# A mixture-of-experts stage: every other weight block issued from ScalarE's queue

## The reference

```python
D_EXPERT = 7 * D_MODEL // 2

def swiglu(t, w_gate, w_up, w_down):
    return (jax.nn.silu(t @ w_gate) * (t @ w_up)) @ w_down

def moe_swiglu(t, router, w_gate, w_up, w_down):
    logits = (t @ router).astype(jnp.float32)
    top_logits, top_idx = lax.top_k(logits, TOP_K)
    gates = jax.nn.softmax(top_logits, axis=-1)
    combine = jnp.sum(jax.nn.one_hot(top_idx, N_EXPERTS, dtype=jnp.float32) * gates[..., None], axis=1)
    out = jnp.zeros_like(t)
    for e in range(N_EXPERTS):
        out = out + combine[:, e:e + 1].astype(t.dtype) * swiglu(t, w_gate[e], w_up[e], w_down[e])
    return out
```

## Time and profile before

| | us |
|---|---|
| median of three executions | 3119.86 (3119.49 to 3123.53) |
| the profiled execution | 3112.41 |
| its span | 3110.6 |
| the first expert begins (TensorE's first unit) | 2019.2 |
| TensorE busy in the span | 2810.8 (90%) |
| DVE, ScalarE busy in the span | 1739.6, 1419.2 |
| DMA engines' share on SP's queue, whole span | 49.9% |

### The profile page before, as it was taken

How to read it: one execution, slowest core, us unless ns; L and a number is a source line. 1 busy time by engine, 2 the same in 40 slices (tenths; PEclk the granted TensorE clock), 3 DMA queues, 4 the chain that set the end, 5 groups by cost and what they waited for, 6 DMA issues and landing times.

```text
span 3110.6 us, 38240 instructions
## 1 busy us (share of the span) xinstructions
PE 2810.8 (90%) x15246; PEld 2269.4 (73%) x15246; DVE 1739.6 (56%) x1787; ACT 1419.2 (46%) x1567; POOL 29.7 (1%) x40
## 2 busy tenths in 40 slices
PE   6989889999887998767679998799999999999997
PEld 4865378854776998667469996687778777777786
DVE  3234265510444775432345445387878878788786
ACT  3234143300343554311134444376766767676675
POOL 0000000000010000000000000000000000000000
PEclk9999999999999999877689999899999999999998
DMA  7447122211332444300015441298989989898895
GB/s 310 183 183 271 54 83 107 90 66 71 112 122 75 150 158 154 112 1 1 16 66 189 159 181 56 95 353 298 351 322 330 343 304 358 302 345 328 324 348 214
DMA packets 84932, 589.78 MB, mean 190 GB/s; under 512 B 9936, under 2 KB 10064, under 8 KB 21328
## 3 DMA queue, kind: packets, MB, share of 16 engines
q1 hardware_dynamic: 83376, 576.16, 49.9%
q10 hardware_dynamic: 1440, 11.93, 1.0%
HBM read 587.01 MB, written 1.05 MB: 189 GB/s over the span
## 4 chain that ended last, share of the span: by engine, by line
PE 82%; DVE 9%; ACT 4%; issue 2%; DMA 2%; ACTq 0%; DVEq 0%; POOL 0%; SPq 0%; POOLq 0%
PE banks L449 24%; PE banks L443 19%; PE banks L444 19%; PE banks L445 19%; DMA ring<-in_stream 2%; DVE ring_rounded L505 1%; ACT ring_rounded L495 1%; DVE ring_rounded L2611 1%; PE banks L2449 1%; DVE rstd L696 1%; DVE activations L1256 0%; PE banks L772 0%; ACT scratch L836 0%; DVE nmax L808 0%; DVE aT L709 0%
## 5 line engine op out<-in xcount | busy, mean ns | idle before, releaser
L444 PE MATMUL banks<-ring_rounded,activations_rounded 128*128 128x512 f32 x1344 | 530.7, 395 | 0.0
L505 DVE TENSOR_TENSOR ring_rounded<-ring,ring_rounded 128x2048 fp32r<-128x2048 f32 (+3 forms) x150 | 302.7, 2022 | 394.3 <-ACT ring_rounded L495 393.4
L444 PE MATMUL banks<-aT_rounded,ring_rounded 128*128 128x256 f32 (+1 forms) x1552 | 500.8, 323 | 0.0
L495 ACT ACTIVATE ring_rounded<-ring 128x2048 fp32r<-128x2048 f32 (+3 forms) x150 | 253.7, 1695 | 324.1 <-PE banks L445 309.3
L444 PEld LDWEIGHTS banks<-aT_rounded,ring_rounded 128*128 128x128 f32 x1552 | 301.3, 194 | 20.8
L443 PE MATMUL banks<-aT_rounded,ring_rounded 128*128 128x256 f32 x960 | 276.5, 288 | 20.9 <-DVE aT_rounded L718 11.6
L444 PEld LDWEIGHTS banks<-ring_rounded,activations_rounded 128*128 128x128 f32 x1344 | 254.7, 190 | 53.6
L445 PE MATMUL banks<-aT_rounded,ring_rounded 128*128 128x256 f32 x960 | 274.8, 286 | 0.0
L2611 DVE TENSOR_TENSOR ring_rounded<-ring,tables_rounded 128x2048 fp32r<-128x2048 f32 x112 | 253.6, 2287 | 27.8 <-ACT tables_rounded L2534 27.5
L2611 DVE TENSOR_TENSOR ring_rounded<-ring,aT_rounded 128x2048 fp32r<-128x2048 f32 x112 | 254.2, 2288 | 19.1 <-ACT aT_rounded L2534 18.9
L2534 ACT ACTIVATE tables_rounded<-ring 128x2048 fp32r<-128x2048 f32 x112 | 215.1, 1921 | 107.5 <-DMA ring<-in_stream 96.7
(11 more groups left out here) (290 smaller groups left out, 5075.3 us busy)
## 6 DMA issues: line engine op xcount, KB each, us to landing
ring<-in_stream SPq DMA_DIRECT2D x491, 1024.0 KB, 5.3
ring<-in_stream SPq DMA_DIRECT2D x48, 704.0 KB, 5.5
ring<-in_stream SPq DMA_DIRECT2D x28, 768.0 KB, 6.4
activations<-in_rpb ACTq DMA_DIRECT2D x2, 1536.0 KB, 6.3
tables<-in_tab_b ACTq DMA_DIRECT2D x1, 2436.0 KB, 8.6
tables<-in_tab_a ACTq DMA_DIRECT2D x1, 2304.0 KB, 8.4
hT<-in_h ACTq DMA_DIRECT2D x1, 2048.0 KB, 15.5
ring<-in_stream SPq DMA_DIRECT2D x4, 512.0 KB, 6.2
```

Source lines behind the costliest of these rows:

```text
L444: pe.matmul(out, exact(upper), exact(w_lower), start=False, stop=False)
L495: act.activation(exact(upper), w, ACT.Copy).then_inc(g.s["act_pieces"], 1)
L505: dve.tensor_tensor(exact(w), w, rounded(upper), ALU.subtract).then_inc(g.s["dve_pieces"], 1)
```

## The change

ScalarE's `split(u)` for even u now issues the DMA of unit n = u + 1, once TensorE has finished unit u - 6, which is unit n - 7. The two waits of `split` have changed places: first TensorE's, then the issue, then the landing of unit u. SyncE issues one unit more ahead of the loop (unit 5), and in the loop only the even units, 6 to 46. The line numbers of `experts_act` behind the new lines move by five.

```diff
         def split(u):
 
-            act.wait_ge(g.expert_in[u % EXPERT_RING], 16 * (u // EXPERT_RING + 1) + it * (16 * UNITS // EXPERT_RING))
             if u >= UPPERS:
                 act.wait_ge(s["pe_experts"], g.at("unit", u - UPPERS) + it * Q)
             else:
                 act.wait_ge(s["pe_experts"], g.at("unit", UNITS + u - UPPERS) - Q + it * Q)
+            if u % 2 == 0:
+
+                n = u + 1
+                src = g.io["stream"][bass.ds(e * ES + (g.expert_base + n // 2), 1), :, UNIT:2 * UNIT]
+                act.dma_start(g.units[n % EXPERT_RING], src.rearrange("a p n -> p (a n)")).then_inc(g.expert_in[n % EXPERT_RING], 16)
+            act.wait_ge(g.expert_in[u % EXPERT_RING], 16 * (u // EXPERT_RING + 1) + it * (16 * UNITS // EXPERT_RING))
             act.activation(exact(g.upper[u % UPPERS]), g.units[u % EXPERT_RING], ACT.Copy).then_inc(s["act_split"], 1)
@@ experts_sp
-    for u in range(AHEAD):
+    for u in range(AHEAD + 1):
 
         sp.wait_ge(*g.moment(("used", base - 1 - (base - 1 - u // 2) % RING)))
         sp.dma_start(g.units[u], g.io["stream"][base + u // 2, :, UNIT * (u % 2):UNIT * (u % 2) + UNIT]).then_inc(g.expert_in[u], 16)
@@
         it = r * NE + e
-        for u in range(AHEAD, UNITS + AHEAD):
+        for u in range(AHEAD + 1, UNITS + AHEAD, 2):
             if u < EXPERT_RING:
```

## The result

| | before | after |
|---|---|---|
| median | 3121.38 us (four executions, 3119.49 to 3123.53) | 3174.12 us (four, 3157.82 to 3175.79) |
| ratio | | 1.0157, 95% interval 1.0123 to 1.0192 |
| the profiled execution, its span | 3112.41, 3110.6 us | 3175.79, 3174.0 us |

By the ratio the changed kernel is slower by 49 us (38 to 60 us); the two medians lie 53 us apart. The direction was forecast, the size was not: 3285 us with a range from 3180 us was too high.

What follows compares the result with a forecast made beforehand. TensorE was taken to set the pace, with ScalarE right behind the transfers. Chained odd transfers cost 23.2 us an expert, times eight 185.6, less 6.6 reserve: 179 us, giving 3285 us (range 3180 to 3370).

Steps and rivals of the forecast that it cites:

- The mechanism: In ScalarE's list, each odd unit's issue waits for the previous odd unit's landing, forming a chain of 7.58 us steps.
- h: On ScalarE, hold from an odd unit's landing to the next odd issue: 0.10 plus some 0.20 us, 0.3 us a step.
- Rival A: Odd and even transfers keep alternating in the expert stage, so not slower: 3120 us within 5 us; chance 0.09.
- Rival B: ScalarE's issues wait for the running ACTIVATE's end: steps of 7.5 us, landings near 5.3 us, 3318 us; chance 0.08.
- 21 steps x 7.58: One expert's odd transfers, all chained and nearly coinciding with even ones: 159.2 us before corrections.
- about two steps run alone: In TensorE's 11.5 us of pauses an expert, two steps are 2.0 us cheaper each: -4.1 us.
- that is where they settle: Odd and even transfers on the two queues stay nearly coincident, odd 0.5 us behind even, at steps of 7.58 us.
- rival C: The chain slips only in part of each expert, pauses restoring alternation: steps of some 6.8 us, 3181 us; chance 0.12.
- The sum's upper bound: Two fully side-by-side transfers land in 7.8 us, a step at most 8.1 us: +259 us in all.
- No margin: Alternation of odd and even transfers needs steps of 5.5 us or less; a slip lengthens the next landing and slip.
- The reserve of 6.6 us: The seven-place ring's 19.25 us less a unit's 12.6 us way: lateness up to 6.6 us costs nothing.
- The clock: TensorE's granted clock may fall in some of its waits; named but given no size.

Runs made afterwards that it cites:

- e2_early: The changed kernel with each odd unit's issue two cuts earlier in ScalarE's list, ahead of the wait for the previous odd unit's landing; 3119.2 us, ratio 1.0011.
- x_after: The changed kernel with ScalarE's last result of an expert and DVE's lower half of group 5 moved one cut forward; 3177.0 us.
- p_after: The changed kernel with seven extra float32 matmuls on TensorE ahead of group 4 of each expert, a pause of about 6 us in weight use; 3173.1 us.
- e4_late: The changed kernel with each odd unit issued behind the cut of the even unit ahead of it; 3271.5 us, ratio 1.0511.
- r6_before: The kernel before with six places for units in the ring instead of seven; 3174.2 us, ratio 1.0180.
- p_before: The kernel before with seven extra float32 matmuls on TensorE ahead of group 4 of each expert; 3166.1 us, ratio 1.0155.
- e3_onequeue: The changed kernel with even units too issued by ScalarE in the split of the unit before, none by SyncE in the loop; 3135.2 us, ratio 1.0058.

## Why the prediction was wrong

**What held.** The mechanism: the odd issues follow the landing of the odd unit before, 0.25 us behind it (h was 0.3); the issue itself is free under a running cut (0.34 us each, e2_early); SyncE's saved issues bring nothing; the order of the waits costs nothing. The queues share the engines, and three steps of the first expert with both in phase are 7.9, 7.2 and 7.1 us, where 7.58 was worked out. Rival A fell by the interval. Rival B fell by the issue times: they come 0.23 us behind the cut's start. The prediction had also named landings of 5.3 us in a slow stage as the sign of B, and that sign would have misled.

**The step that failed** is the sum for one expert, "21 steps x 7.58", with "about two steps run alone". It let TensorE's pauses shorten two steps and then go on with the coinciding phase, because "that is where they settle". The runs show in its place that they do not settle. Behind each pause the odd units start in alternation, at landings near 5.0 us. The slip grows over some units, steps of 7 us and more come in the middle of a stretch, and then the steps shrink again; in the first expert this goes with the odd issues moving ahead of the even ones, by 0.1, 0.2 and 0.7 us. Of the 96 steps between the odd units 7 to 31 in the profile after, 21 reach 7 us: six in the first expert (up to unit 27), five in the third, none in the seventh. Their mean is 6.3 us, not 7.58. x_after (shorter pauses, some 100 us of loss) agrees, and so does p_after (one pause more, 7 us), with the reservation made there. e4_late, at +159 us, came near the forecast's loss of 165 us with steps of 6.6 us in the mean there and not 7.58, so it does not bear out the sum.

This was rival C, 3181 us, with a chance of 0.12, and it should have been the forecast, for the pauses stood in the earlier trace rows and the alternating phase was already known to be possible. That C's time is so near (3174 us) is in part luck: its 6.8 us was put halfway between two bounds, and it left out the reserve's error and the clock, below.

The sum's upper bound failed too. It gave a landing 7.8 us and a step 8.1 us at most, with two transfers sharing; unit 17 took 9.2 us and the longest step, in the third expert, 10.0 us. When unit 17 went out at 2060.84 us, two even units were under way, one until 2062.93 us and one since 2060.40 us, and a third went out at 2066.41 us, before either had landed. So at times three transfers ran side by side.

**"No margin".** The prediction held that alternation can't last, since a step of 5.6 us is longer than 5.5 us. Expert 7 ran whole in 132.9 us. That the 0.4 us of transposes behind every fourth unit and the pauses just carry it, and that small differences decide whether an expert slips, is an inference: no run here tests it.

**The reserve of 6.6 us** was the second error, and of the other sign. It counts for the matmuls that use a unit, not for jobs that stand in the same list behind cuts of units needed 10 us later. r6_before took 2.75 us of it and lost 56 us. In the changed kernel 18 of the 41 us of new idle time are at such a join, L2481. In four experts (the second, fourth, fifth and eighth) it waits 2.9 to 6.2 us, against 2.4 us at most before, while no unit's weights come late.

**The clock** was left unpriced: some 50 us more at the lower level, and TensorE's work in the stage took 16 us longer.

What stays open: why x_after's loss is as large as 100 us, what decides in which expert the slip begins, and why the odd issues get ahead of the even ones again. None was tried.

## What to carry to other kernels

In this kernel a DMA issued from a compute engine inherited every wait ahead of it in that engine's list. Where one of them is the landing of an earlier transfer of its stream, that stream has one transfer under way at a time, however many places the ring has, and the issue belongs ahead of that wait or on an engine with nothing else to do. Count a ring's reserve at the first job that stands behind the prefetched work in a list, not at the one that uses the data. And before multiplying a worked-out step by all steps, ask what resets it.

## What the runs showed that was not expected

- Extra work can be nearly free: p_after carries the 51 us that p_before adds, and is 57 us (50 to 65) over the kernel before where the changed kernel is 49 us (38 to 60).
- A chained stream in one queue keeps landings of 5.3 us in the median (e3_onequeue); the same chain beside a second queue reaches 9.6 us. The long landings are those of transfers that ran beside one or two of the other queue.
- Two short waits of TensorE an expert, 2.8 and 2.3 us, were worth 49 us over the eight: 34 us of idle time, and 15 us of matmul time that the clock gave back.
